# Output projection begun inside the last recurrent rounds, its weights asked for earlier, and the first key projection interleaved with the forget projection

## The chip, the cores and the metric

The kernel runs on one core of a Trainium2 chip. The metric is the device time of one execution in microseconds (us). TensorE (PE) does the matmuls and its sequencer the waits for them, VectorE (DVE) and ScalarE (ACT) do the elementwise work and read the results out of PSUM, GpSimd (POOL) scales weights and starts some transfers, and SyncE (SP) only starts transfers. Each engine runs its own instruction list in order, and the lists meet at semaphores.

## The reference, cut to what matters

```python
def rwkv7_layer(h, ...):
    xn = rmsnorm(h, norm)
    proj = token_shift(xn @ w_in, mu)              # r, k, v, z, two small ones
    ...
    y = wkv7_scan(r, decay, k, v, kk, a)           # recurrence over 1040 tokens, 16 heads of 64
    y = group_norm_per_head(y) * gn_w + gn_b
    out = (y + bonus) * silu(z)
    return h + out @ w_out                         # the output projection, then the residual

def shared_kv(h, kv_norm, kv_w, kv_f_bias, k_norm):
    kvf = rmsnorm(h, kv_norm) @ kv_w               # [k | v | 16 forget logits]
    k_sh = head_rmsnorm(kvf[..., :D], k_norm)
    v_sh = kvf[..., D:2 * D]
    log_f = log_sigmoid(kvf[..., 2 * D:] + kv_f_bias)
    c_all = cumsum(log_f, axis=1)
    return k_sh, v_sh, c_all

def fox_layer(h, k_sh, v_sh, c_all, ...):
    proj = rmsnorm(h, norm) @ w_in                 # q and z
    ...                                            # softmax(q k / 8 + c[t] - c[s]), causal, times v
    return h + (attn * silu(z)) @ w_out
```

D is 1024, the sequence has 1024 tokens and 16 meta tokens (1040 in all, padded to 1044), everything is float32. There is one recurrent layer and one attention layer.

## The kernel before

A float32 operand x is split into a high part xh (rounded to the type fp32r) and a low part xl = x - xh, likewise a weight into wh and wl, and a product of 128 channels is three matmuls: wh xh, wl xh, wh xl. The 1044 columns are taken as three segments of 348, so one channel block k (of KO = 8) against one output tile is nine matmuls, and one output tile is 72. `products` writes them. High parts are made by ScalarE (`split_hi`, `split_row`), low parts by VectorE (`split_lo`, `split_row`), and VectorE raises `w_lo` or `x_lo` when a weight or a row block is usable. Raw weights arrive in the two buffers of `wr`, asked for by SyncE in `load_w`, which waits until the previous content of the buffer has been split.

**The recurrent layer** is worked off for 8 pairs of heads times 4 segments of time, in rounds. `round_order` writes the steps of a round as one list, and every engine walks that list and picks its own work. A full round holds projections for the segment after the next, the triangular inverse of the next one ("p", "x"), and the state chain ("chain", one small matmul pair, one VectorE step, and again) of the one before. Three draining rounds follow the last full one. In the second of them, `round_order(1, False, False, True, False, False)`, only this is left: chain steps 1 to 3 of the last segment (the third is empty there), "y", the two matmul groups of the group norm "gn1" and "gn2", and "rsqrt" (Ln and Exp on ScalarE). The last round finishes the group norm on VectorE ("gn3") and stores the last segment.

A finished pair of heads is stored to `oa_scr` in DRAM. SyncE reads it back as row block k of the output projection's input (`osq`, two buffers) and it is split by `split_row`. Blocks 0 to 6 are split during the last full round ("orow" steps in `last_round_order`); block 7 only exists when the last segment is stored.

**The output projection** (tiles N_AO to N_AO + 7) starts behind the last round. Tiles 0 and 1 run side by side, channel block by channel block, in the PSUM groups G (banks 0 to 2 and 3 to 5). For tiles 2 to 7 a tile takes the buffer of the tile two before it: when tile m is finished, VectorE adds the residual (`h_t`, read back from `xt_scr`) and then splits the weight of tile m + 2. SyncE's list there is: eight loads of osq, eight loads of `h_t` (two in flight), and then the weights of tiles 2 to 7.

**Behind it** the sum of squares for the norm is closed (`over`), `normalise(1)` writes eight row blocks one after the other, and TensorE multiplies each by the 16 forget columns (tile N_F, nine matmuls for each row block, only 16 wide). Then the forget chain runs: logit, Abs, Exp, Ln, min, subtract, the cumulative sum, scale, high part, low part, alternately on VectorE and ScalarE, 16 partitions wide. GpSimd stores both parts to `c_scr` and sets the extra rows of the key and query buffers. `first_round` is the list of the steps before attention starts: key projection ("proj", 0, i), its head norm ("sumsq", "rsq", "norm"), the same for the query, "stackk", "stackq", value, and the row maxima ("smax"). Its products alternate between two PSUM banks (B_G), and ScalarE must read a bank out before the next but one product can start.

## Time and profile before

| | us |
|---|---|
| runs shown (3) | 2131.5, 2128.23, 2131.59 |
| median | 2131.5 |
| profiled execution, device time | 2133.43 |
| its span, first to last instruction | 2131.6 |
| mean granted TensorE clock, share of full | 0.966 |

TensorE is busy 92% of the span, VectorE 49%, ScalarE 44%, GpSimd 11%. The span lies 1.8 us under the profiled execution's own time. The part that the change touches lies between 1036 and 1285 us of the span: the last full recurrent round ends near 1065, the three draining rounds near 1096, tiles 0 and 1 of the output projection end at 1120, tile 7 at 1194, the first query projection at 1264. Read there which engine waits and which wait ends last; busy shares of the whole span say little about it.

### The profile page before, as it was taken

Reading aid. Unit: us, or ns where it says so; the run is one execution under the profiler, and the core shown is the slowest. Engines: PE = TensorE matmul, PEld = TensorE weight load, DVE = VectorE, ACT = ScalarE, POOL = GpSimd, SP = SyncE. Lnnn points to the kernel's source line nnn. Section 1 sums busy time; section 2 is a strip of 40 time slices with the busy share of each in tenths; the row PEclk is TensorE's granted clock in tenths of the full one; section 3 lists DMA queues with packets and bytes.
Section 4 is the critical chain, followed back from the end, with each engine's and each line's share of the span. In section 5 each row is a group of like instructions: output and inputs, shape, how many; then the busy total and the mean of one; then the engine's idle time right before and its main releaser. Section 6 shows DMA issues by size and latency. Waiting matters only on the chain.

```text
span 2131.6 us, 56907 instructions
## 1 busy us (share of the span) xinstructions
PE 1964.1 (92%) x24895; PEld 1684.4 (79%) x24895; DVE 1051.4 (49%) x1991; ACT 943.6 (44%) x1677; POOL 234.2 (11%) x261
## 2 busy tenths in 40 slices
PE   6699999999999999999889789999999999999798
PEld 4588888889898888889779577777777877777477
DVE  2646565666656665665623543343343533443521
ACT  2445454444444444454412253544555364444621
POOL 0011111111111111111000021001010101100000
PEclk9799999999999999999869898999999999999799
DMA  5101000010101000010231210010110110110233
GB/s 201 50 2 42 11 25 27 18 38 5 47 8 37 15 27 27 12 41 8 77 108 52 101 42 21 26 30 21 35 26 26 35 31 21 30 35 16 79 114 118
DMA packets 103738, 89.92 MB, mean 42 GB/s; under 512 B 4101, under 2 KB 95864, under 8 KB 103240
## 3 DMA queue, kind: packets, MB, share of 16 engines
q1 hardware_dynamic: 100120, 68.50, 10.9%
q0 software_dynamic: 3168, 17.14, 2.5%
q8 instruction: 199, 3.26, 0.6%
q10 hardware_dynamic: 208, 0.66, 0.1%
q14 instruction: 43, 0.35, 0.1%
HBM read 64.96 MB, written 21.33 MB: 40 GB/s over the span
## 4 chain that ended last, share of the span: by engine, by line
PE 74%; DVE 9%; ACT 9%; issue 5%; DMA 2%; SPq 0%; ACTq 0%; DVEq 0%; POOLq 0%
PE ps L1711 6%; PE ps L2024 6%; PE ps L2026 5%; PE ps L2025 5%; PE ps L1713 5%; PE ps L1712 5%; PE ps L2107 5%; PE ps L1815 4%; PE ps L1647 3%; PE ps L1649 3%; PE ps L1648 3%; PE ps L1844 2%; PE ps L2060 2%; PE ps L2088 2%; PE ps L1839 2%
## 5 line engine op out<-in xcount | busy, mean ns | idle before, releaser
L1711 PE MATMUL ps<-xh,wh 128*128 128x258 f32 (+1 forms) x1024 | 328.0, 320 | 7.5 <-ACT arena L887 3.5
L1712 PE MATMUL ps<-xh,wl 128*128 128x258 f32 (+1 forms) x1024 | 291.2, 284 | 0.0
L1713 PE MATMUL ps<-xl,wh 128*128 128x258 f32 (+1 forms) x1024 | 291.0, 284 | 0.0
L2024 PE MATMUL ps<-xh,wh 128*128 128x348 f32 x768 | 262.3, 341 | 8.4 <-ACT arena_b L1075 5.2
L2025 PE MATMUL ps<-xh,wl 128*128 128x348 f32 x768 | 248.5, 324 | 0.0
L2026 PE MATMUL ps<-xl,wh 128*128 128x348 f32 x768 | 248.3, 323 | 0.0
L1711 PEld LDWEIGHTS ps<-xh,wh 128*128 128x128 f32 x1024 | 193.6, 189 | 26.0 <-ACT arena L887 6.0
L1591 DVE TENSOR_REDUCE arena_b<-ps 128x1 f32<-128x144 f32 (+4 forms) x224 | 106.2, 505 | 192.8 <-PE ps L2064 176.3
L1712 PEld LDWEIGHTS ps<-xh,wl 128*128 128x128 f32 x1024 | 194.3, 190 | 2.6
L1713 PEld LDWEIGHTS ps<-xl,wh 128*128 128x128 f32 x1024 | 193.6, 189 | 0.0
L1075 ACT ACTIVATE arena_b<-ps 128x348 f32<-128x348 f32 x96 | 43.9, 458 | 293.8 <-PE ps L2026 293.8
L2107 PE MATMUL ps<-arena_b 128*128 128x512 f32 (+4 forms) x448 | 164.3, 483 | 4.7 <-ACT arena_b L1160 4.7
L858 ACT ACTIVATE arena<-ps,pp 128x257 f32<-128x257 f32 (+1 forms) x128 | 61.3, 479 | 230.1 <-PE ps L1713 230.1
L1647 PE MATMUL ps<-xh,wh 128*128 128x348 f32 (+2 forms) x368 | 133.0, 361 | 28.2 <-DVE xl L1208 21.3
L2024 PEld LDWEIGHTS ps<-xh,wh 128*128 128x128 f32 x768 | 146.7, 191 | 13.8 <-ACT arena_b L1075 5.5
L2025 PEld LDWEIGHTS ps<-xh,wl 128*128 128x128 f32 x768 | 146.3, 190 | 4.5 <-issue 0.3
L2026 PEld LDWEIGHTS ps<-xl,wh 128*128 128x128 f32 x768 | 145.8, 190 | 0.0
L1200 DVE TENSOR_TENSOR wl<-wr,wh 128x1024 fp32r<-128x1024 f32 (+1 forms) x50 | 60.1, 1204 | 154.8 <-ACT wh L1038 98.7
L1648 PE MATMUL ps<-xh,wl 128*128 128x348 f32 (+2 forms) x368 | 131.4, 357 | 0.0
L1649 PE MATMUL ps<-xl,wh 128*128 128x348 f32 (+2 forms) x368 | 131.2, 357 | 0.0
L1408 DVE TENSOR_TENSOR arena<-ps,levels 128x256 f32<-128x256 f32 (+1 forms) x192 | 86.9, 452 | 78.3 <-PE ps L1815 77.4
L1815 PE MATMUL ps<-arena 64*64 64x64 f32 x2880 | 121.1, 226 | 2.9 <-DVE arena L1421 2.9
(255 smaller groups left out, 4357.4 us busy)
## 6 DMA issues: line engine op xcount, KB each, us to landing
wr<-in_w_in SPq DMA_DIRECT2D x33, 512.0 KB, 4.1
xt_scr<-arena POOLq DMA_DIRECT2D x2, 4176.0 KB, 13.3
wr<-in_kv_w SPq DMA_DIRECT2D x16, 512.0 KB, 3.9
wr<-in_b_w_in SPq DMA_DIRECT2D x16, 512.0 KB, 3.9
arena<-xt_scr SPq DMA_DIRECT2D x8, 522.0 KB, 4.7
arena<-oa_scr SPq DMA_DIRECT2D x8, 520.0 KB, 3.7
arena<-in_x SPq DMA_DIRECT2D x8, 512.0 KB, 3.4
wr<-in_w_out SPq DMA_DIRECT2D x8, 512.0 KB, 3.8
```

Of the source, the lines that this page charges most:

```text
L1591: dve.tensor_reduce(mpart[:, 3 * t + part:3 * t + part + 1], ps[:, B_SM[i % 2], 0:k1 - k0], AX.X, ALU.max).then_inc(S.smax, 1)
L1647: pe.matmul(acc, wh[:, slot, k, 0:width], xh[:, k, t], start=(k == 0), stop=False)
L1648: pe.matmul(acc, wl[:, slot, k, 0:width], xh[:, k, t], start=False, stop=False)
L1649: mm = pe.matmul(acc, wh[:, slot, k, 0:width], xl[:, k, t], start=False, stop=(k == KO - 1))
L1711: pe.matmul(bank, wh[:, j, k, :], xh[:, k, t], start=(k == 0), stop=False)
L1712: pe.matmul(bank, wl[:, j, k, :], xh[:, k, t], start=False, stop=False)
L1713: mm = pe.matmul(bank, wh[:, j, k, :], xl[:, k, t], start=False, stop=(k == KO - 1))
L1815: mm = pe.matmul(ps[to[c], B_P, x * CH:(x + 1) * CH], am_[hc, e, j, A_BA], xs[hc, 0, x, :] if l else ident[hc, hc], start=(l > 0), stop=Tr ...
L2024: pe.matmul(bank[:, 0:SEG], wh[:, slot, k, :], xh[:, k, t], start=(k == 0), stop=False)
L2025: pe.matmul(bank[:, 0:SEG], wl[:, slot, k, :], xh[:, k, t], start=False, stop=False)
L2026: mm = pe.matmul(bank[:, 0:SEG], wh[:, slot, k, :], xl[:, k, t], start=False, stop=(k == KO - 1))
L2107: pe.matmul(ps[:, B_PV[qb_], q0 - 512 * qb_:512], vflat[e][0:n_k, kt, :], pt[n_ % 4][0:n_k, 0:n_q], start=(kt == 0), stop=(kt == 4 * qb_ + 4),
```

## The change

There are four edits.

- `tail_order` puts 14 pieces ("ao", m, k) into the second draining round: channel blocks 0 to 6 of output tiles 0 and 1, nine matmuls each. One stands behind each of the steps chain 1, chain 2, chain 3, "y" and "gn1", the other nine at the round's end. Only channel block 7 of both tiles is left behind the rounds. The output projection uses the banks GO (1 to 3 and 4 to 6), so that banks 0 and 7 stay with the recurrence.
- SyncE asks for the weights of tiles 2 and 3 behind the osq loads 3 and 4, not behind the eight loads of `h_t`.
- The first key projection leaves `first_round` on TensorE and runs with the forget projection, row block by row block, three segments in banks 0 to 2. Its weight is split before `normalise(1)` on both engines.
- The forget chain is a step of `first_round` now, behind the key's head norm. GpSimd scales the value weight before it waits for the chain's end, not after it.

```diff
+        def tail_order():
+            pieces = [("ao", m, k) for k in range(KO - 1) for m in range(2)]
+            steps = []
+            for st_ in round_order(1, False, False, True, False, False):
+                steps.append(st_)
+                if st_[0] in ("chain", "y", "gn1"):
+                    steps.append(pieces.pop(0))
+            return steps + pieces
@@ SyncE
                 sync.dma_start(osq[k % 2][:, 0:T], oa_scr[k][:, 0:T]).then_inc(O_LOADED[k % 2], 16)
+                if k in (3, 4):
+                    n = N_AO + k - 1
+                    load_w(n, wo[:, :, (k - 1) * P:k * P], n % 2, n)
...
-            for m in range(2, KO):
+            for m in range(4, KO):
                 load_w(N_AO + m, wo[:, :, m * P:(m + 1) * P], (N_AO + m) % 2, N_AO + m)
@@ GpSimd
             scale_b(0, 1)
+            scale_b(0, 2)
             pool.wait_ge(S.c_lo, 1)
@@ ScalarE (VectorE alike)
             split_hi(n % 2, None, 1, n - 1, H)
+            split_hi((N_B + 0) % 2, None, 2, N_B - 2)
             normalise(1)
-            split_hi((N_B + 0) % 2, None, 2, N_B - 2)
-            act.wait_ge(S.f_logit, 1)
...
+                    elif kind == "forget":
+                        act.wait_ge(S.f_logit, 1)
...
@@ TensorE
+                    elif kind == "ao":
+                        m, k = st_[1:]
...
+                        pe.wait_ge(S.x_lo, KO + k + 1)
+                        products(GO[(N_AO + m) % 2], (N_AO + m) % 2, channels=[k])
...
-            pe.wait_ge(S.w_lo, N_F + 2)
+            pe.wait_ge(S.w_lo, N_B + 2)
+            pe.wait_ge(S.h_ln, 2)
             for k in range(KO):
                 pe.wait_ge(S.x_lo, 2 * KO + k + 1)
                 mm = products(G[N_F % 2], N_F % 2, H, channels=[k])
...
+                for i in range(3):
+                    t = slice(i * SEG, (i + 1) * SEG)
+                    pe.matmul(G[0][:, i, :], wh[:, N_B % 2, k, :], xh[:, k, t], start=(k == 0), stop=False)
+                    pe.matmul(G[0][:, i, :], wl[:, N_B % 2, k, :], xh[:, k, t], start=False, stop=False)
+                    mm = pe.matmul(G[0][:, i, :], wh[:, N_B % 2, k, :], xl[:, k, t], start=False, stop=(k == KO - 1))
@@ first_round
-            return (of(0) + [("sumsq", 0, i) for i in range(3)] + [("rsq", 0), ("norm", 0)]
+            return (of(0) + [("sumsq", 0, i) for i in range(3)] + [("rsq", 0), ("norm", 0), ("forget",)]
```

Lines of the changed kernel lie some 17 further down on TensorE. TensorE's list in the second draining round, before the change (L1932 is a chain step, L1944 "y", L1955 and L1962 the group norm, L1647 the first matmul of the output projection; a row with "waits" waits for those semaphores):

```order
L1932 MATMUL ps<-arena 64x64 [waits s_ready]
L1932 MATMUL ps<-arena 64x64
L1944 MATMUL ps<-arena 64x64 [waits s_ready,rp_ready]
L1944 MATMUL ps<-arena 64x64 x7
L1955 MATMUL ps<-arena,head_ones 128x256 [waits y_added]
L1962 MATMUL ps<-arena,head_ones 128x256 [waits gn_sq,gn_centred]
L1647 MATMUL ps<-xh,wh 128x348 [waits gn_centred,x_lo,gn_rstd,w_lo]
```

The same place of the changed kernel, to the end of "gn2" (L1949 is a chain step, L1961 "y", L1980 and L1987 the group norm, L1664 the first of nine matmuls of a piece, of which the other eight are left out each time):

```order
L1949 MATMUL ps<-arena 64x64 [waits s_ready]
L1949 MATMUL ps<-arena 64x64
L1664 MATMUL ps<-xh,wh 128x348 [waits x_lo]
...
L1664 MATMUL ps<-xh,wh 128x348 [waits x_lo]
...
L1961 MATMUL ps<-arena 64x64 [waits s_ready,rp_ready]
L1961 MATMUL ps<-arena 64x64 x7
L1664 MATMUL ps<-xh,wh 128x348 [waits x_lo]
...
L1980 MATMUL ps<-arena,head_ones 128x256 [waits y_added]
L1664 MATMUL ps<-xh,wh 128x348 [waits x_lo]
...
L1987 MATMUL ps<-arena,head_ones 128x256 [waits gn_sq,gn_centred]
```

So five pieces stand inside the chain and the group norm, and the wait for the group norm's end (gn_rstd) moved behind all fourteen.

ScalarE's list from the closing of the norm's statistics, before the change (L793 a weight's high part, L806 and L808 the norm's Ln and Exp, L811 the row blocks, L1026 to L1032 the forget chain, L1075 reading a projection out, L1089 the Ln behind "sumsq"):

```order
L793 ACTIVATE wh<-wr 128x8x16 [waits proj_done,w_scaled]
L806 ACT_TABLE_LOAD [waits setup_dve]
L811 ACTIVATE xh<-arena 128x1044 [waits xn_mul] x8
L793 ACTIVATE wh<-wr 128x1024 [waits proj_done,w_scaled]
L1026 ACTIVATE arena_b<-arena_b 16x1044 [waits f_logit]
L1028 ACTIVATE arena_b<-arena_b 16x1044 [waits f_abs]
L1032 ACTIVATE wh<-arena_b 16x1044 [waits c_scaled]
L793 ACTIVATE wh<-wr 128x1024 [waits proj_done,w_scaled]
L1075 ACTIVATE arena_b<-ps 128x348 [waits b_done] x3
L1089 ACTIVATE arena_b<-ps,cst 128x348 [waits b_done] x3
```

The same of the changed kernel (L807 a weight's high part, L825 the row blocks, L1082 reading a projection out, L1096 the Ln, L1109 to L1115 the forget chain, L1044 the value weight's high part):

```order
L807 ACTIVATE wh<-wr 128x1024 [waits proj_done,w_scaled]
L825 ACTIVATE xh<-arena 128x1044 [waits xn_mul] x8
L1082 ACTIVATE arena_b<-ps 128x348 [waits b_done] x3
L1096 ACT_TABLE_LOAD
L1096 ACTIVATE arena_b<-ps,cst 128x348 [waits b_done] x3
L1109 ACTIVATE arena_b<-arena_b 16x1044 [waits f_logit]
L1111 ACTIVATE arena_b<-arena_b 16x1044 [waits f_abs]
L1115 ACTIVATE wh<-arena_b 16x1044 [waits c_scaled]
L1044 ACTIVATE wh<-wr 128x1024 [waits b_done,w_scaled]
L1082 ACTIVATE arena_b<-ps 128x348 [waits b_done] x3
```

The forget chain moved from ahead of reading out the key projection to ahead of reading out the query projection.

## Rows read from the trace of the kernel before

**Rows 1.** The page's first part: engine, busy us, share, instructions.

```profile
PE 1964.1 (92%) x24895; PEld 1684.4 (79%) x24895; DVE 1051.4 (49%) x1991; ACT 943.6 (44%) x1677; POOL 234.2 (11%) x261
```

**Rows 2.** Windows: from:to, us, each engine's busy us (instructions), PEclk, DMA share, GB/s.

```profile
1085.51:1091.31 5.80, 3.29 (x26) 2.09 (x27) 2.65 (x7) 0.54 (x2) 0.54 (x1) 0.50 0.07 24
...
1094.84:1099.33 4.49, 4.49 (x16) 4.49 (x17) 1.33 (x3) 0.00 (x0) 0.54 (x1) 0.50 0.09 33
1099.33:1120.08 20.75, 20.75 (x130) 20.46 (x129) 2.49 (x2) 1.08 (x1) 0.00 (x0) 1.00 0.85 270
...
1123.78:1126.55 2.77, 2.77 (x9) 2.77 (x10) 2.76 (x3) 1.67 (x2) 0.00 (x0) 0.50 0.59 168
...
1136.85:1194.30 57.45, 57.36 (x360) 57.07 (x359) 17.04 (x15) 9.65 (x9) 0.40 (x1) 1.00 0.11 29
```

**Rows 3.** Timeline of TensorE: start, us, line, operation, operands, [idle before, releaser].

```profile
1085.51 0.48 PE L1932 MATMUL ps<-arena 64*64 64x64 f32 x4 [0.47 <-DVE arena L1452]
...
1091.31 1.19 PE L1962 MATMUL ps<-arena,head_ones 128*128 128x256 f32 x2 [1.06 <-ACT arena L984]
```

**Rows 4.** Chain of waits, 1000 to 1300: "y" and "gn1" in a full round.

```profile
1019.74 0.42 PE ps L1944 x16
...
1023.24 0.66 PE ps L1955 x2
```

**Rows 5.** Chain of waits, 1087 to 1124: start, us, what; then VectorE's timeline.

```profile
1096.54 2.03 DMA oa_scr<-arena
...
1099.48 5.27 DMA arena<-xt_scr
...
1114.45 6.93 DMA wr<-in_w_out
...
1103.30 1.25 DVE L1296 TENSOR_TENSOR xl<-arena,xh 128x1044 fp32r<-128x1044 f32 x1 [7.06 <-ACT xh L838]
```

**Rows 6.** Timeline of VectorE behind tile 2: residual, then a weight's low part.

```profile
1136.88 1.25 DVE L1507 SCALAR_TENSOR_TENSOR arena<-ps,arena 128x1044 f32<-128x1044 f32 x1 [9.62 <-PE ps L1649]
1138.04 1.22 DVE L1200 TENSOR_TENSOR wl<-wr,wh 128x1024 fp32r<-128x1024 f32 x1
```

**Rows 7.** Timeline of TensorE: first matmul of tile 2 of the output projection.

```profile
1123.78 0.66 PE L1647 MATMUL ps<-xh,wh 128*128 128x348 f32 x1 [3.69 <-DVE wl L1200]
```

**Rows 8.** Chain of waits in the last full round: osq load 4.

```profile
1050.71 3.86 DMA arena<-oa_scr
```

**Rows 9.** Timelines of TensorE, VectorE (twice) and GpSimd at the norm's first row blocks.

```profile
1210.74 0.45 PE L1647 MATMUL ps<-xh,wh 128*16 128x348 f32 x1 [7.36 <-DVE xl L1208]
...
1210.63 2.83 DVE L1217 TENSOR_TENSOR arena<-arena 128x1044 f32<-128x1044 f32 x1
1213.38 1.23 DVE L1208 TENSOR_TENSOR xl<-arena,xh 128x1044 fp32r<-128x1044 f32 x1
...
1210.30 2.05 POOL L666 TENSOR_TENSOR wr<-wr,params 128x1024 f32<-128x1024 f32 x1 [12.00 <-DMA wr<-in_b_w_in]
```

**Rows 10.** Timelines of ScalarE (forget chain, key, query) and TensorE.

```profile
1231.28 1.08 ACT L1026 ACTIVATE arena_b<-arena_b 16x1044 f32<-16x1044 f32 x1 [3.58 <-DVE arena_b L1525]
...
1248.37 0.46 ACT L1075 ACTIVATE arena_b<-ps 128x348 f32<-128x348 f32 x1 [5.37 <-PE ps L2026]
...
1254.30 1.08 ACT L1103 ACTIVATE arena_b<-arena_b 128x1044 f32<-128x1044 f32 x1
...
1263.91 0.46 ACT L1075 ACTIVATE arena_b<-ps 128x348 f32<-128x348 f32 x1 [3.35 <-PE ps L2026]
...
1265.49 1.28 ACT L1089 ACT_TABLE_LOAD   x1
...
1242.71 0.64 PE L2024 MATMUL ps<-xh,wh 128*128 128x348 f32 x1 [5.21 <-ACT arena_b L1075]
```

**Rows 11.** Timelines of GpSimd (last of eight memsets) and ScalarE's queue ("stackk").

```profile
1251.52 1.87 POOL L753 MEMSET qc<- 1x1044 f32 x2
...
1268.93 0.48 ACTq L1117 DMA_DIRECT2D kb<-c_scr  x1
```

More of the change, by code:

```diff
@@ L762, in store_ob @@
                 pool.sem_inc(S.ob_free, 1)
-            for j in range(2, 4):
-                scale_b(0, j)
+            scale_b(0, 3)
             scale_b(1, 0)
@@ L1995, in _ @@
                     pe.wait_ge(S.res_added, m - 1)
[L1996 removed]
+                products(GO[n % 2], n % 2).then_inc(S.proj_done, 1)
             pe.wait_ge(S.res_added, KO)
@@ L2009, in round_pe @@
                     kind = st_[0]
+                    if first and st_[0:2] == ("proj", 0):
+                        continue
                     if kind in ("proj", "sumsq", "vrow"):
@@ L2013, in round_pe @@
                         bank = ps[:, B_G[local % 2], :]
-                        if not (first and local < L_K + 2) and st_[3:] != (1,):
+                        if st_[3:] != (1,):
                             pe.wait_ge(S.b_evac, chunk(p, local) - 1)
```

81 lines of the change are left out of this document (43 added, 38 removed).

## The prediction

> **What bounds the kernel now.** First the page's first part: TensorE is busy 92% of the span [rows 1]. The 8% left is where a change of order can pay, so the second view is the timeline of TensorE with what ended its idle times, and the third is the chain of waits at those places. Between 1085 and 1264 us there are three holes. The first is the draining rounds: a chain step lasts 0.48 and TensorE then waits 0.47 for VectorE, the group norm waits for ScalarE [rows 3], and the output projection starts only at 1094.84, at the low clock. The second is tile 2's weight: TensorE waits 3.69 [rows 7], because the weight was asked for at 1114.45, behind the residual's loads, and took 6.93 to land [rows 5]. The third is the forget chain: ScalarE works it off in its order and cannot read the key projection out, so TensorE waits 5.21 for a bank [rows 10].
>
> The windows give two prices for a 348-column matmul. At a granted clock of 0.50 (1.2 GHz) 16 take 4.49 and 9 take 2.77: 0.29 each. At 1.00 (2.4 GHz) 360 take 57.45: 0.16 each. After 1094.84 the clock rose 4.5 after the dense matmuls began, after 1123.78 2.8 after [rows 2]. I take 4.4.
>
> **Part one, the 14 pieces.** They remove nothing, 126 matmuls only move. Before, tiles 0 and 1 end at 1120.08 [rows 2]. After, on the same clock of the trace: the second chain step starts at 1085.51 [rows 3], the first piece 0.2 behind it. Three pieces (27 matmuls) and a chain step are 15 at 0.29, 12 at 0.16 and 0.2: 6.5, to 1092.2. "y" 0.42 [rows 4], a piece 1.44, "gn1" 0.66 [rows 4], a piece 1.44, "gn2" 0.66: to 1096.8. Each of these steps waits for VectorE or ScalarE, but those waits (0.47, 1.06) are shorter than a piece. Before, "gn2" ended at 1092.5 [rows 3]. So the group norm's end, the store and the reload come 4.3 later: channel block 7 is ready at 1104.55 + 4.3 = 1108.9 [rows 5]. Meanwhile nine pieces (81 x 0.16 = 13.0) run until 1109.8, so block 7 is just covered, by 0.9. Its two parts end at 1111.2 and 1112.7.
>
> **Part two, the weight of tile 2.** It is there now, so behind tile 0 only residual and low part stand: from 1136.85 to 1139.26, 2.4 [rows 2, 6]. Tile 2 starts at 1113.6, after an idle time of 0.9 in place of 3.69, and I take its clock as still up: 72 x 0.16 = 11.5, end 1125.1. Before it ended at 1136.85 [rows 2]. Gain of both parts: 11.7. What is late next: h_t's first load, asked for 4.3 later, lands at 1099.48 + 5.27 + 4.3 = 1109.1 [rows 5], 2.1 ahead of its use at 1111.2. The weights of tiles 4 and 5 come some 4 later than h_t's last load did, but TensorE needs tile 4's only after tiles 2 and 3, 23.0 behind 1113.6. Both have cover.
>
> The cost is in the last full round, where SyncE's queue now has tile 2's weight ahead of osq load 4. That load is on the chain of waits there with its whole 3.86 [rows 8], and ScalarE stands in order behind it. From above: an equal load asked for just behind another took 5.27 in place of 3.86 [rows 5, 8], 1.4 more. From below nothing, since the weight goes out some 3.4 earlier and may be through. Nothing makes the load faster, so no gain. I take the middle, 0.7, since 3.4 of lead is near a transfer's 3.86 but short of it. Tile 3's weight meets osq loads 5 and 6, which stand under the same bound. Gain so far 11.0.
>
> **Part three, the key projection with the forget projection.** Before, TensorE starts the forget blocks at 1210.74 [rows 9] and ScalarE reads out the last key segment at 1248.37 [rows 10]. After, each row block brings 18 matmuls: the first costs 15 x 0.29 + 3 x 0.16 = 4.8, to 1215.6; the others 2.9 each, more than the 2.4 in which VectorE makes a block, so TensorE is the bound. Block 1 was ready at 1213.38 + 1.23 = 1214.6 [rows 9]. There is a clash: GpSimd's scaling from 1210.30 to 1212.35 stretched VectorE's multiply to 2.83 [rows 9], ending 1.1 behind it, and the value weight's scaling (2.05) now follows at once. Block 1 comes at 1216.7, the eighth is multiplied at 1216.7 + 7 x 2.88 = 1236.8.
>
> The Trainium skill, GPSIMD Engine Reference, Specifications, says that GpSimd shares its SBUF interfaces with VectorE and contends with instructions of two SBUF inputs. That speaks against moving this scaling, and the stretched multiply of [rows 9] agrees. Without it the sum of this part would be 1.1 better (1215.6 + 7 x 2.88 = 1235.7).
>
> ScalarE splits the query weight in between (1.06), and ends reading out at 1237.7 against 1248.83: 11.1 earlier. The norm's Ln now needs a table load that the forget chain's Ln paid for before; 1.28 less the 1.0 that "sumsq" takes: 0.3. The key's Exp ends at 1255.38 - 10.8 = 1244.6 [rows 10]. Now the forget chain stands: from its Abs to TensorE's restart 11.43 (1231.28 to 1242.71), so 1256.0. Meanwhile TensorE has done two query segments (48 x 0.16 = 7.7, from 1252.4 - 10.8 = 1241.6, where 1252.4 is the restart behind "sumsq", 4.0 behind the readout of [rows 10]) and waits 6.7 for a bank. The third, at the low clock as the key's was (1242.71 to 1248.37, 5.66), ends at 1261.7 in place of 1263.9 [rows 10]. The stall was moved, not removed: of 10.8 gained 2.2 stay, and 0.3 more, as the query's Ln finds its table (a load of 1.28 at 1265.49, partly covered). Part three: 2.5; bounds 1.0 and 4.0 (a longer clash; none, and a faster rise).
>
> The end of the chain also moves GpSimd's stores and eight memsets: before done at 1253.4 [rows 11], 10.7 behind TensorE's restart of [rows 10], now about 1266.7. ScalarE's "stackk" asks for them at 1268.93 - 2.5 = 1266.4 [rows 11]: no cover where there were 15, but ScalarE's data path is at the query's Exp for some 2 more, so I cost it at nothing. The scaling of the query layer's last weight, queued on GpSimd behind the memsets, has cover of the same size.
>
> **Sum.** 11.0 + 2.5 = 13.5. The profiled execution took 2133.43, which gives 2119.9; it lay 1.9 above the median 2131.5, on which the prediction stands: 2118.0.
>
> **The rivals.**
> 1. *The key's gain is wholly lost.* The forget chain or GpSimd's memsets are a little later than worked out, and "stackk" waits, with ScalarE's reading out behind it. For: the memsets have a cover of about 2 where they had 15. Against: value products give ScalarE some slack. Gain 11.0: 2120.5.
> 2. *The clock rises only behind "gn2".* For: it stood at 0.50 from 1085.51 to 1091.31 with TensorE busy for 3.29 of 5.80 [rows 2], and small steps lie between the first pieces. Then the 45 matmuls of the first five pieces cost 13.1 in place of 9.2 (15 at 0.29, 30 at 0.16), and "y", "gn1", "gn2" twice their 1.7: 5.6 later for all behind. Against: nothing idles between the pieces. Gain 13.5 - 5.6 = 7.9: 2123.6.
> 3. *Slower than before.* The clock stays at 1.2 GHz through all pieces: 144 x 0.29 and 3.7 for the small steps are 45.5 from 1085.7, to 1131.2 in place of 1112.7, and tile 2's first ten at 0.29 cost 1.3 more: 19.8 lost, against 13.5. Time 2131.5 + 6.3 = 2137.8. It turns from gain to loss when the rise comes later than 30 us after the forecast one (13.5 / 0.45, the share that a low clock costs). Against it: the same matmuls got 1.00 after 4.5 [rows 2].
> 4. *More than forecast.* The osq load isn't delayed, no clash, the clock rises after 2.8 as at 1123.78: 0.7, 1.1 and 1.6 x 0.45 = 0.7 more, a gain of 16.0: 2115.5.
> 5. *The change doesn't do what it says*: tile 2's weight is early only if the buffer is free and no wait holds SyncE. Its wait is for a split long done, so I fold this into rival 2.
>
> **How the numbers follow.** Forecast 0.62, rival 1 0.17, rival 2 0.10, rival 3 0.04, rival 4 0.07. The forecast's own band is its bounds: 11.0 plus or minus 0.7 and 1.0 to 4.0, so 2115.8 to 2120.2, and the runs themselves spread 3.4. From 2114.0 to 2122.5 the range holds the forecast, rival 1 and most of rival 4; it leaves out rivals 2 and 3 and a little of the others, 0.2 at most. A measurement of this kernel can tell about 0.2%, 4.3 us, from no change. Only rival 3 is slower; rivals 1 and 2 together (gain 5.4) with an unlucky spread could come within: faster 0.92, same 0.04, slower 0.04.
>
> **What the profile after would show.** Chain steps 0.2 to 3 apart with L1664 between them; a granted clock of 1.00 from about 1090; no idle time over 0.5 before block 7; tile 2's first matmul about 10 earlier, with an idle time near 1 and released by VectorE's low part. At the norm 18 matmuls for each row block and nearly no waits. In the query projection an idle time near 6.7 in front of the third segment, released by ScalarE reading out. The prediction is wrong if the clock is at 0.50 behind 1092, if block 7 is waited for, if osq load 4 lands more than 1.4 later, or if the idle time in the query projection is much shorter or longer than 6.7.

## The result and the profile after

The changed kernel takes 2117.0 us (median of 4 runs, 2115.4 to 2118.8), the kernel before, in runs beside it, 2131.2 (2128.2 to 2131.6). The ratio is 0.9935, with a 95% interval of 0.9921 to 0.9949: 14.2 us gained, where 13.5 was forecast. The profiled executions are 2133.43 before and 2118.27 after, with spans of 2131.6 and 2116.5. The 15.1 us between the spans is read below, stretch by stretch. Line numbers of TensorE's products are now L1664 to L1666 (before L1647 to L1649); the residual is L1523 (before L1507), the read-out L1082 (before L1075). The changed kernel was measured once more later, with a trace of its own; it is called the second trace below.

| milestone, us from the span's start | before | after | earlier by |
|---|---|---|---|
| ScalarE reads row 4 of the last full round | 1054.59 | 1054.72 | -0.1 |
| second chain step of the last head round | 1085.51 | 1085.16 | 0.4 |
| tile 2 of the output projection starts | 1123.78 | 1114.40 | 9.4 |
| tile 2's residual on VectorE | 1136.88 | 1126.19 | 10.7 |
| TensorE starts on the normalised input | 1210.74 | 1200.05 | 10.7 |
| third query segment read out | 1263.91 | 1250.71 | 13.2 |

**Part one and two, after.** Windows of the changed kernel, with the columns of [rows 2]: the stretch, each engine's busy time and instructions, the granted clock, the DMA share and GB/s.

```profile
1085.16:1091.08 5.92, 5.92 (x25) 5.31 (x26) 1.87 (x5) 0.00 (x0) 0.13 (x1) 0.50 0.02 4
1091.08:1113.30 22.22, 22.22 (x149) 21.60 (x148) 4.83 (x8) 6.08 (x8) 0.95 (x2) 1.00 0.38 128
1114.40:1126.15 11.75, 11.75 (x73) 11.75 (x74) 3.48 (x3) 1.95 (x2) 0.00 (x0) 1.00 0.84 250
```

Before, the stretch from the same chain step on had TensorE busy for 3.29 of 5.80 us [rows 2]. Now it is busy for all 5.92, though still at 1.2 GHz (a granted clock of 0.50), and from 1091.08 to the end of tile 1 it is busy without a break at 2.4 GHz. Tile 2's 72 matmuls, which began at the low clock before [rows 2], take 11.75.

The timeline of TensorE and VectorE there (start, us, engine and line, operation, operands, idle time before and what ended it):

```profile
1085.16 0.48 PE L1949 MATMUL ps<-arena 64*64 64x64 f32 x4 [0.47 <-DVE arena L1468]
1085.56 0.66 PE L1664 MATMUL ps<-xh,wh 128*128 128x348 f32 x1
...
1088.47 0.48 PE L1949 MATMUL ps<-arena 64*64 64x64 f32 x4
...
1092.96 0.68 PE L1961 MATMUL ps<-arena 64*64 64x64 f32 x16
...
1097.00 0.59 PE L1987 MATMUL ps<-arena,head_ones 128*128 128x256 f32 x2
...
1114.40 0.44 PE L1664 MATMUL ps<-xh,wh 128*128 128x348 f32 x1 [1.04 <-DVE wl L1216]
...
1108.60 1.25 DVE L1312 TENSOR_TENSOR xl<-arena,xh 128x1044 fp32r<-128x1044 f32 x1 [6.95 <-ACT xh L852]
1126.19 1.25 DVE L1523 SCALAR_TENSOR_TENSOR arena<-ps,arena 128x1044 f32<-128x1044 f32 x1 [8.30 <-PE ps L1666]
```

The chain step at 1088.47, "y" at 1092.96 and the second group norm at 1097.00 carry no bracket: TensorE comes to them late enough that nothing is waited for. In [rows 3] the same kinds of steps wait 0.47 and 1.06. Block 7's low part is made at 1108.60 to 1109.85 and TensorE doesn't wait for it. The wait of 3.69 for tile 2's weight [rows 7] is 1.04, ended by the low part L1216, which stands behind tile 0's residual.

**Part three, after.** The norm's first row blocks: TensorE, then VectorE and GpSimd (the place of [rows 9]).

```profile
1200.05 0.45 PE L1664 MATMUL ps<-xh,wh 128*16 128x348 f32 x1 [7.36 <-DVE xl L1224]
...
1201.10 2.94 DVE L1224 TENSOR_TENSOR xl<-arena,xh 128x1044 fp32r<-128x1044 f32 x1
1204.08 2.83 DVE L1233 TENSOR_TENSOR arena<-arena 128x1044 f32<-128x1044 f32 x1
...
1200.04 5.76 POOL L680 TENSOR_TENSOR wr<-wr,params 128x1024 f32<-128x1024 f32 x2 [12.43 <-DMA wr<-in_b_w_in]
```

Beside GpSimd's two scalings, 5.76 together, two of VectorE's operations take 2.94 and 2.83 in place of 1.25. In [rows 9] one scaling stretched one.

ScalarE from the key's norm to the key's copy for the stacking ("stackk"), then TensorE, then GpSimd (the places of [rows 10] and [rows 11]):

```profile
1227.29 1.28 ACT L1096 ACT_TABLE_LOAD   x1
...
1232.88 1.08 ACT L1119 ACTIVATE arena_b<-arena_b 128x1044 f32<-128x1044 f32 x1
1233.86 1.06 ACT L1109 ACTIVATE arena_b<-arena_b 16x1044 f32<-16x1044 f32 x1
...
1242.87 1.07 ACT L1115 ACTIVATE wh<-arena_b 16x1044 fp32r<-16x1044 f32 x1 [4.45 <-DVE arena_b L1575]
...
1250.71 0.46 ACT L1082 ACTIVATE arena_b<-ps 128x348 f32<-128x348 f32 x1 [5.14 <-PE ps L2058]
...
1255.99 0.49 ACTq L1133 DMA_DIRECT2D kb<-c_scr  x1
...
1257.62 1.06 ACT L1135 ACTIVATE ka<-arena_b 64x1044 fp32r<-64x1044 f32 x1
...
1227.41 3.56 PE L2065 MATMUL ps<-arena_b,head_ones 128*128 128x348 f32 x6 [2.02 <-ACT arena_b L1088]
...
1245.28 0.66 PE L2056 MATMUL ps<-xh,wh 128*128 128x348 f32 x1 [6.53 <-ACT arena_b L1082]
...
1254.08 1.88 POOL L768 MEMSET qc<- 1x1044 f32 x2
```

The forget chain begins at 1233.86 behind the key's Exp (1232.88), and within it ScalarE stands idle for 4.45 until VectorE's scan and scaling are through. TensorE gets its bank back at 1245.28, after an idle time of 6.53. The stall of 5.21 [rows 10] was moved, not removed.

**How the spans' 15.1 us add up.** 1.0 lies ahead of anything the change touches (VectorE's last low part of the setup is at 1036.55 before and 1035.56 after). The touched part gives 12.5, with the 0.3 of the query's Ln counted. Another 1.5 comes behind it, in a stretch whose code is the same, by where the clock is low. These are windows of 10 us, the first of the kernel before, the second of the changed one, both beginning at the same instruction:

```profile
1280.32:1290.32 10.00, 9.62 (x54) 8.94 (x55) 1.95 (x5) 1.20 (x4) 1.53 (x1) 0.83 0.00 0
```

```profile
1266.82:1276.82 10.00, 9.63 (x64) 8.94 (x65) 1.95 (x5) 1.20 (x4) 1.90 (x1) 1.00 0.04 11
```

The granted clock is 0.83 in the one and 1.00 in the other, and TensorE gets 54 matmuls done against 64. From the first copy for the key's stacking to the third it is 95.3 before and 93.8 in the changed kernel, but 93.3 in its second trace and 95.3 in a kernel with the same code there (the memsets alone, below). So the 1.5 is chance, and the forecast doesn't claim it.

### The profile page after: what moved, and what is told of

It is laid out like the page before. It is cut to its first block, busy times and chain, and to the rows that moved or that the text cites. A ratio compares the mean times of both kernels' runs of the same rounds, so it can differ in the third digit from the quotient of the medians.

```text
span 2116.5 us, 56909 instructions
## 1 busy us (share of the span) xinstructions
PE 1953.6 (92%) x24895; PEld 1677.9 (79%) x24895; DVE 1053.3 (50%) x1991; ACT 942.9 (45%) x1677; POOL 236.8 (11%) x261
## 4 chain that ended last, share of the span: by engine, by line
PE 75%; ACT 9%; DVE 9%; issue 5%; DMA 2%; SPq 0%; ACTq 0%; DVEq 0%; POOLq 0%
PE ps L1728 6%; PE ps L2056 5%; PE ps L2058 5%; PE ps L2057 5%; PE ps L1730 5%; PE ps L1729 5%; PE ps L2139 5%; PE ps L1832 4%; PE ps L1664 3%; PE ps L1666 3%; PE ps L1665 3%; PE ps L1861 2%; PE ps L2092 2%; PE ps L2120 2%; PE ps L1856 2%
## 5 line engine op out<-in xcount | busy, mean ns | idle before, releaser
L2056 PE MATMUL ps<-xh,wh 128*128 128x348 f32 x744 | 253.9, 341 | 9.8 <-ACT arena_b L1082 6.5
L2057 PE MATMUL ps<-xh,wl 128*128 128x348 f32 x744 | 239.9, 322 | 0.0
L2058 PE MATMUL ps<-xl,wh 128*128 128x348 f32 x744 | 239.8, 322 | 0.0
L1728 PEld LDWEIGHTS ps<-xh,wh 128*128 128x128 f32 x1024 | 193.4, 189 | 26.0 <-ACT arena L901 6.0
L1729 PEld LDWEIGHTS ps<-xh,wl 128*128 128x128 f32 x1024 | 194.2, 190 | 2.6
L1730 PEld LDWEIGHTS ps<-xl,wh 128*128 128x128 f32 x1024 | 193.5, 189 | 0.0
L1082 ACT ACTIVATE arena_b<-ps 128x348 f32<-128x348 f32 x96 | 43.6, 457 | 285.5 <-PE ps L2058 285.5
L2056 PEld LDWEIGHTS ps<-xh,wh 128*128 128x128 f32 x744 | 141.7, 190 | 15.4 <-ACT arena_b L1082 6.8
L1664 PE MATMUL ps<-xh,wh 128*128 128x348 f32 (+2 forms) x368 | 132.2, 359 | 20.4 <-DVE xl L1224 18.5
L2057 PEld LDWEIGHTS ps<-xh,wl 128*128 128x128 f32 x744 | 141.2, 190 | 4.4 <-issue 0.3
L2058 PEld LDWEIGHTS ps<-xl,wh 128*128 128x128 f32 x744 | 140.6, 189 | 0.0
L1216 DVE TENSOR_TENSOR wl<-wr,wh 128x1024 fp32r<-128x1024 f32 (+1 forms) x50 | 60.1, 1205 | 152.7 <-ACT wh L1044 99.1
L1666 PE MATMUL ps<-xl,wh 128*128 128x348 f32 (+2 forms) x368 | 129.8, 353 | 0.0
```

The costliest lines, as they stand in the source:

```text
L1664: pe.matmul(acc, wh[:, slot, k, 0:width], xh[:, k, t], start=(k == 0), stop=False)
L1666: mm = pe.matmul(acc, wh[:, slot, k, 0:width], xl[:, k, t], start=False, stop=(k == KO - 1))
L1728: pe.matmul(bank, wh[:, j, k, :], xh[:, k, t], start=(k == 0), stop=False)
L1729: pe.matmul(bank, wl[:, j, k, :], xh[:, k, t], start=False, stop=False)
L1730: mm = pe.matmul(bank, wh[:, j, k, :], xl[:, k, t], start=False, stop=(k == KO - 1))
L2056: pe.matmul(bank[:, 0:SEG], wh[:, slot, k, :], xh[:, k, t], start=(k == 0), stop=False)
```

## The experiments

Ten runs in three groups, each group measured together with the kernel before on one chip. Four stand beside 2132.7 us for the kernel before: weights behind the residual, no pieces, the key part alone, weights behind load 6. Four stand beside 2131.2: pieces behind the second group norm, the forget chain in two, that with the memsets ahead, and that with two smaller mends. The last two, the memsets alone and the changed kernel again, stand beside 2132.3. I use differences between medians of one group, and traces from the same instruction to the same instruction, since two stretches whose code no edit changes vary by 2 to 3.5 us (last section).

### What the early weights, the pieces and their place are worth

**Weights behind the residual again.** The pieces and the key part stay.

```diff
-                if k in (3, 4):
-                    n = N_AO + k - 1
-                    load_w(n, wo[:, :, (k - 1) * P:k * P], n % 2, n)
...
-            for m in range(4, KO):
+            for m in range(2, KO):
```

> The changed kernel, but the weights of output tiles 2 and 3 are asked for behind the eight residual loads again. Theory: the pieces alone are worth nothing or worse, because they delay the group norm by about 5 us, with it the residual loads, and tile 2's weight stands behind those. The last residual load is asked for at about 1119.3 on the changed kernel's clock, the weight takes 6.9 to land, then 2.3 for its high and low part: tile 2 starts near 1128.6 in place of 1114.4, and starts at the low clock (1.3 more), while osq load 4 lands 0.6 earlier. So about 15 slower than the changed kernel, near 2132, no faster than the kernel before. Rival: the pieces carry most of the gain by themselves and the early weight only its own stall of 2.8 and a cold start of 1.3: then about 4 slower than the changed kernel, near 2121.

Measured: 2135.1 (12 runs, 2129.6 to 2139.6), ratio 1.0005 (0.9996 to 1.0014). ScalarE, TensorE and SyncE's transfer (chain of waits) in this kernel:

```profile
1127.14 1.06 ACT L804 ACTIVATE wh<-wr 128x1024 fp32r<-128x1024 f32 x1 [19.09 <-DMA wr<-in_w_out]
...
1129.51 0.66 PE L1661 MATMUL ps<-xh,wh 128*128 128x348 f32 x1 [16.73 <-DVE wl L1213]
```

```profile
1119.44 7.68 DMA wr<-in_w_out
```

TensorE is done with tiles 0 and 1 as early as in the changed kernel, and then waits 16.73 us. Worse, the weight is asked for at 1119.44, 35.0 behind the second chain step (1084.46 here), where before it was 28.9 behind it [rows 3, 5]. The pieces delay the group norm's end, with it the last load of its rows, and with that everything that stands behind this load on SyncE. By the traces, the stretch from the second chain step to TensorE's start on the normalised input is 133.2 here and 125.2 before. So the pieces without the early weights lose 8 us there. Part of it comes back behind it, where the key part brings its gain.

**No pieces, early weights kept.** The output projection's first two tiles run behind the group norm as before (their waits and products move back there on TensorE, not shown), the rest is as changed.

```diff
-            pieces = [("ao", m, k) for k in range(KO - 1) for m in range(2)]
-            steps = []
-            for st_ in round_order(1, False, False, True, False, False):
-                steps.append(st_)
-                if st_[0] in ("chain", "y", "gn1"):
-                    steps.append(pieces.pop(0))
-            return steps + pieces
+            return round_order(1, False, False, True, False, False)
```

> The changed kernel without the pieces: channel blocks 0 to 6 of tiles 0 and 1 stand behind the rounds and behind the wait for the group norm again. The early weights and the key part stay. Theory: tiles 0 and 1 end near 1119.4 in place of 1113.3, tile 2 follows after 1 us, so 6 to 6.5 slower than the changed kernel: near 2123.3. Rival (early weight is all there is, the pieces are hidden by the wait for channel block 7): within 1 of the changed kernel.

Measured: 2124.3 (5 runs), ratio 0.9960 (0.9947 to 0.9973). TensorE at tile 2:

```profile
1118.13 0.43 PE L1658 MATMUL ps<-xh,wh 128*128 128x348 f32 x1 [1.04 <-DVE wl L1210]
```

From its second chain step (1082.41) to tile 2 it takes 35.7, against 29.2 in the changed kernel and 38.3 before: the pieces are worth 6.5 there, as expected.

**The key part alone.** Both edits above together.

> The kernel before with the key part alone (key projection beside the forget one, forget chain as a step behind the key's norm, value weight scaled earlier); neither pieces nor early weights. Theory: the stall only moved to the query projection, 2.5 to 2.8 faster than the kernel before: near 2128.5. Rival (the key projection's earlier end counts in full): 10 or more faster, near 2121; second rival (nothing comes through): within 0.7 of the kernel before.

Measured: 2130.6 (11 runs), ratio 0.9990 (0.9982 to 0.9999), 2.0 us below the kernel before in the same group, where 2.5 to 2.8 was expected. In its trace the stretch from TensorE's start on the normalised input to its restart for the third query segment is 45.5 (1207.35 to 1252.82), against 45.2 in the changed kernel.

With these three the parts can be added up, all in one group: key part alone 2130.6; with the early weights 2124.3, so 6.3 for the weights; with the pieces too 2119.5 (the run with the weights behind load 6, below, which differs from the changed kernel only in where they are asked for), so 4.8 for the pieces. But with the pieces and late weights it is 2135.1: there the pieces cost 4.5. Their sign hangs on the weights. By the traces the weights' share is smaller than by the medians: from the second chain step to the start on the normalised input the weights bring 3.3 (124.7 to 121.4). Of this 1.8 is tile 2's start, and the rest is tile 2 itself, whose first 3 us have a granted clock of 0.54 with the late weight and 1.00 with the early one. The two profiled executions differ by 3.6 in all, since the one of the key part alone is the fastest of its 11 runs. The rest of the 6.3 I can't place; the two ratios' intervals leave 3 us of room on either side.

**All pieces behind the second group norm**, instead of between its steps.

```diff
                 steps.append(st_)
-                if st_[0] in ("chain", "y", "gn1"):
-                    steps.append(pieces.pop(0))
             return steps + pieces
```

> All 14 pieces stand directly behind the second group norm instead of between the chain steps, y and the first group norm; nothing else differs from the changed kernel. Theory (the pieces pay twice: they fill TensorE's waits and they lift its clock before the group norm): the group norm ends some 4.5 us earlier than in the changed kernel, as before the change (1092.5 against 1097.0), but the first pieces then run at the low clock with nothing hidden, so tiles 0 and 1 end later: 14 pieces from 1092.5 with 4.5 us of clock rise are 16 x 0.29 + 110 x 0.16 = 22.2 us, to 1114.8, then block 7's 18 matmuls 2.9, to 1117.7, against 1113.4 in the changed kernel. So some 4 us slower than the changed kernel: near 2121, ratio to the kernel before 0.9953. Rival (the place does not matter, only that they run before block 7 is there): within 1 us of the changed kernel, ratio 0.9935. Against no pieces at all (2124.3, ratio 0.9960) the theory expects 2 to 3 us faster.

Measured: 2119.7 (5 runs), ratio 0.9947 (0.9933 to 0.9961). TensorE:

```profile
1083.27 0.33 PE L1947 MATMUL ps<-arena 64*64 64x64 f32 x4 [0.52 <-DVE arena L1466]
...
1115.83 0.43 PE L1662 MATMUL ps<-xh,wh 128*128 128x348 f32 x1 [1.04 <-DVE wl L1214]
```

32.6 from the second chain step to tile 2: 3.3 more than the changed kernel, 3.2 less than without pieces. (The seven traces with the pieces between the steps and the weights early lie between 28.1 and 29.3.) So about half of the pieces' gain is that they run while block 7 is on its way through memory, and half that they stand between the chain steps. How much of that second half is filled waits and how much is an earlier rise of the clock, no run takes apart. The rival, that the place doesn't matter, falls in the trace; the ratios alone (0.9947 and 0.9935) would not tell.

### The transfer that the early weights delay

**Weights asked for behind load 6** of the group norm's rows, instead of behind loads 3 and 4.

```diff
-                if k in (3, 4):
-                    n = N_AO + k - 1
-                    load_w(n, wo[:, :, (k - 1) * P:k * P], n % 2, n)
+                if k == 6:
+                    for n in (N_AO + 2, N_AO + 3):
+                        load_w(n, wo[:, :, (n - N_AO) * P:(n - N_AO + 1) * P], n % 2, n)
```

> The changed kernel, but the weights of tiles 2 and 3 are asked for behind osq load 6, where no osq load follows for some 45 us. Theory: osq load 4 lands after 3.9 in place of 4.7, the last full round is 0.6 to 0.8 shorter, all behind is earlier by that: 0.7 faster than the changed kernel, near 2116.4; ScalarE's wait for osq load 4 falls from 1.05 to about 0.2. Rival (that load's delay is covered): ScalarE's wait falls and the time stays.

Measured: 2119.5 (6 runs, 2113.3 to 2121.1), ratio 0.9931 (0.9919 to 0.9943). Too near 0.9935 to tell. The timeline of ScalarE tells it: row 1's and row 4's copies, first in the kernel before, then in the changed one, then in this one.

```profile
1044.59 1.06 ACT L838 ACTIVATE xh<-arena 128x1044 fp32r<-128x1044 f32 x1
...
1054.59 1.07 ACT L838 ACTIVATE xh<-arena 128x1044 fp32r<-128x1044 f32 x1 [0.20 <-DMA arena<-oa_scr]
```

```profile
1043.88 1.06 ACT L852 ACTIVATE xh<-arena 128x1044 fp32r<-128x1044 f32 x1
...
1054.72 1.08 ACT L852 ACTIVATE xh<-arena 128x1044 fp32r<-128x1044 f32 x1 [1.05 <-DMA arena<-oa_scr]
```

```profile
1045.65 1.06 ACT L852 ACTIVATE xh<-arena 128x1044 fp32r<-128x1044 f32 x1
...
1055.73 1.07 ACT L852 ACTIVATE xh<-arena 128x1044 fp32r<-128x1044 f32 x1 [0.28 <-DMA arena<-oa_scr]
```

10.00, 10.84 and 10.08 from the one to the other. The weight ahead of load 4 costs 0.84 there, and behind load 6 it costs nothing. All twelve traces agree: 10.8 to 11.2 in the seven with the weights behind loads 3 and 4, 9.8 to 10.1 in the five others. The cost reaches the chain nearly whole. From row 1 to the second chain step the three take 40.92, 41.28 and 40.94, but over all twelve traces it is 41.2 to 42.0 with the weights there (mean 41.5) and 40.4 to 40.9 without (mean 40.8), so some 0.7. That is below what a comparison of whole runs can show.

### The stall that was moved

In the changed kernel the next thing in the way is the forget chain. Behind it stand two waits: ScalarE can't read out the first query segment while it waits for VectorE's scan, and the key's stacking waits for GpSimd, whose stores and eight memsets follow the chain's end. Four kernels take these apart: the chain cut in two, the memsets moved, both, and neither.

**The forget chain in two.** ScalarE's last copy and VectorE's low part become a step of their own behind the first query segment's read-out.

```diff
             return (of(0) + [("sumsq", 0, i) for i in range(3)] + [("rsq", 0), ("norm", 0), ("forget",)]
-                    + of(1) + [("sumsq", 1, i) for i in range(3)] + [("rsq", 1), ("norm", 1)]
+                    + proj(1, 0) + [("forget2",)] + proj(1, 1) + proj(1, 2) + [("sumsq", 1, i) for i in range(3)] + [("rsq", 1), ("norm", 1)]
...
                         act.activation(f_a[0:H, :], f_a[0:H, :], ACT.Ln, bias=1.0).then_inc(S.f_ln, 1)
+                    elif kind == "forget2":
                         act.wait_ge(S.c_scaled, 1)
...
+                    elif kind == "forget2":
                         dve.wait_ge(S.c_hi, 1)
```

> The forget chain is cut in two steps: ScalarE's last copy (which waits 4.45 us for VectorE's scan) and VectorE's low part stand behind the first query segment's read-out, so that ScalarE reads the segment out first. Theory: TensorE's idle time of 6.5 us before the third query segment falls to about 1.1 us, but nearly all of that is given back at the next wait: ScalarE then stands before the key's stacking, which waits for GpSimd's eight memsets (they end at 1256.0 in the changed kernel, behind the forget chain's end). Gain 1 us: near 2116, ratio 0.9930. Rival (the idle time of TensorE is itself the loss): 5 to 7 us faster than the changed kernel, near 2111, ratio 0.9905.

Measured: 2116.6 (5 runs), ratio 0.9938 (0.9924 to 0.9951). TensorE, ScalarE and GpSimd:

```profile
1238.57 0.43 PE L2058 MATMUL ps<-xh,wh 128*128 128x348 f32 x1 [1.13 <-ACT arena_b L1082]
...
1255.96 1.07 ACT L1136 ACTIVATE ka<-arena_b 64x1044 fp32r<-64x1044 f32 x1 [5.98 <-POOL qc L768]
...
1253.52 1.87 POOL L768 MEMSET qc<- 1x1044 f32 x2
```

TensorE's idle time falls from 6.53 to 1.13, and next to nothing comes of it: ScalarE now waits 5.98 for the memsets, with the next weight and its read-outs queued behind. This copy comes 56.5 behind TensorE's start on the normalised input, 1.1 earlier than in the changed kernel's first trace (57.6) and 2.2 earlier than in its second (58.7), and the ratio shows no gain. The rival, that TensorE's idle time is itself the loss, is ruled out.

**The same, with the memsets ahead** of GpSimd's wait for the chain's low part.

```diff
-            pool.wait_ge(S.c_lo, 1)
-            pool.dma_start(c_scr[:, 0, :], f32(chi[0:H, :])).then_inc(S.c_stored, 16)
-            pool.wait_ge(S.c_stored, 16)
-            pool.dma_start(c_scr[:, 1, :], f32(clo[0:H, :])).then_inc(S.c_stored, 16)
             pool.wait_ge(S.h_stored, 16)
...
             pool.wait_ge(S.setup_bp, 8)
+            pool.wait_ge(S.c_lo, 1)
+            pool.dma_start(c_scr[:, 0, :], f32(chi[0:H, :])).then_inc(S.c_stored, 16)
+            pool.wait_ge(S.c_stored, 16)
+            pool.dma_start(c_scr[:, 1, :], f32(clo[0:H, :])).then_inc(S.c_stored, 16)
             pool.wait_ge(S.c_stored, 32)
```

> As e5_forget_in_two, and GpSimd's eight memsets stand ahead of its wait for the forget chain's low part instead of behind its two stores. Theory: the key's stacking then waits only for the two stores (the second lands near 1250 on the changed kernel's clock), which is no later than the query's norm, so the gain of the cut is kept: the key's copy at 1251.7 in place of 1257.6, 5 to 6 us faster than the changed kernel: near 2111.5, ratio 0.9908. Rival (memsets beside VectorE's work of 1224 to 1236 stretch its operations as GpSimd's scaling does, and the key's norm or the query's low weight comes later): 2 us or less faster than the changed kernel.

Measured: 2108.0 (4 runs, 2105.5 to 2111.0), ratio 0.9893 (0.9878 to 0.9909). That is 8.6 below the kernel with the cut alone.

```profile
1238.18 0.43 PE L2058 MATMUL ps<-xh,wh 128*128 128x348 f32 x1 [1.12 <-ACT arena_b L1082]
...
1223.04 1.87 POOL L764 MEMSET qc<- 1x1044 f32 x2
...
1249.80 1.08 ACT L1136 ACTIVATE ka<-arena_b 64x1044 fp32r<-64x1044 f32 x1 [0.21 <-issue]
```

The memsets are over by 1225, where nobody needed GpSimd, and ScalarE's copy for the key's stacking follows the Exp directly. From TensorE's start on the normalised input to this copy it takes 51.5 (1198.35 to 1249.80), 56.5 in the run before it and 57.6 in the changed kernel (1200.05 to 1257.62): 6.1 less. The rival, a clash of the memsets with VectorE, was hardly put to the test: from 1217.46 to 1224.91, while they ran, VectorE had three short operations, which took 1.29, 0.54 and 0.54 as in the changed kernel.

**The memsets alone**, the forget chain whole.

> The changed kernel with GpSimd's eight memsets ahead of its wait for the forget chain's low part, and the forget chain whole. Theory (the cut and the memsets' place pay only together: the two waits stand in parallel ahead of the key's stacking): the memsets' end at 1256.0 was hidden behind the query's norm, which ends there by the third query segment's lateness, so moving it alone brings at most the 0.6 us by which the rows leave room: within 1 us of the changed kernel, ratio 0.993 to 0.9935. Rival (the memsets were the bound by themselves, and the cut adds little): most of the 6 us of the two together, ratio near 0.991.

Measured: 2118.4 (5 runs), ratio 0.9933 (0.9919 to 0.9947).

```profile
1242.67 0.66 PE L2056 MATMUL ps<-xh,wh 128*128 128x348 f32 x1 [6.63 <-ACT arena_b L1082]
...
1256.31 1.07 ACT L1135 ACTIVATE ka<-arena_b 64x1044 fp32r<-64x1044 f32 x1
```

TensorE's idle time is the changed kernel's, and the copy comes 58.5 behind the start on the normalised input (1197.84), which is within what the changed kernel does (57.6 and 58.7). The copy follows the query's Exp, and that waits for the third query segment.

**The changed kernel again**, as the base in the same group.

> The changed kernel itself, unchanged, beside the same runs of the kernel before, as the base that e8_memsets_alone is compared with on one chip. Theory and rival alike: ratio within the interval of the first measurement, 0.9921 to 0.9949, so near 0.9935. Its trace tells how much of a stretch's length comes from where the clock rises: the first pieces should again stand at 1.2 GHz for 4 to 6 us, and the last pair's attention may be up to 3.5 us longer or shorter than in the first trace.

Measured: 2119.4 (5 runs), ratio 0.9939 (0.9926 to 0.9953). So the memsets alone bring 1.0 by the medians, which their spread doesn't tell from nothing, the cut alone nothing by its ratio (0.9938), and both together some 9 to 10 by the ratios and 6 to 7 by the traces up to the key's copy. Two waits ran beside each other and ended within a us; only taking both away moves the end. In the first trace the stacking is issued at 1255.99, right when the memsets are over (1255.96). In the second they are over at 1255.73 and it is issued at 1256.68, so there the third query segment is the later one. The rest of the 9 to 10 isn't explained: the last stretch of the kernel, whose code is the same, is 3.5 us shorter in the traces of all three kernels with the chain in two (last section).

The third segment of the two traces, its window from TensorE's restart to the read-out, the first trace first:

```profile
1245.28:1250.71 5.43, 5.39 (x24) 5.10 (x24) 1.19 (x1) 0.29 (x2) 3.23 (x5) 0.73 0.47 121
```

```profile
1245.06:1251.97 6.91, 6.88 (x24) 6.59 (x24) 1.18 (x1) 0.29 (x1) 4.72 (x7) 0.55 0.38 95
```

The same 24 matmuls take 5.43 at a granted clock of 0.73 and 6.91 at 0.55.

**With two smaller mends**: the weights behind load 6, and the third scaling on GpSimd behind the norm's last low part, so that one scaling and not two meets VectorE there (only the second is shown).

```diff
             scale_b(0, 1)
-            scale_b(0, 2)
             pool.wait_ge(S.h_stored, 16)
             pool.wait_ge(S.x_lo, 3 * KO)
+            scale_b(0, 2)
             pool.wait_ge(S.w_scaled, 4)
```

> As e6_memsets_ahead, and two smaller mends: the weights of tiles 2 and 3 are asked for behind load 6 of the group norm's rows in place of loads 3 and 4 (ScalarE waited 1.05 us for load 4 in place of 0.20), and the third scaling on GpSimd stands behind the last low part of the normalised input, so that only one scaling clashes with VectorE's work there. Theory: 0.8 + 0.3 to 0.5 us faster than e6_memsets_ahead: near 2110.5, ratio 0.9903. Rival: the load's wait lies beside other work, then no more than 0.3 us from e6_memsets_ahead.

Measured: 2107.5 (4 runs, 2107.3 to 2108.8), ratio 0.9890 (0.9875 to 0.9905). From TensorE's start on the normalised input to the copy for the key's stacking it is 50.4, 1.1 less than the kernel with the cut and the memsets ahead, and from the setup's last low part to the second chain step 49.2 in place of 50.2. But the ratio can't tell the two apart. By the ratios this version is 23.4 us below the kernel before and 9.6 below the changed one.

## Why the prediction was right, step by step

**The first pieces: direction and mechanism right, 1.1 us too early.** The pieces fill the waits and the clock rises among them, as said. It didn't stay low until "gn2" (rival 2) or through all pieces (rival 3). But "y" comes 7.8 behind the second chain step (1085.16 to 1092.96), where 6.7 was worked out. The term that was mis-sized is "15 at 0.29, 12 at 0.16 and 0.2". The clock rose 5.5 behind the first piece, not 4.4, so 17 matmuls ran at the low clock (the window's 25 instructions less the 8 of two chain steps): 0.3. The other 0.8 is at the seams: the first piece starts 0.40 behind its chain step and the next one 0.41 behind 1088.47, where 0.2 was taken for each, and a piece's first matmul holds TensorE for 0.46 (1085.56 to 1086.02) in place of 0.29. From "y" to the end of the second group norm it is 4.6, as worked out.

**Cover of block 7: right, but thin.** It was ready 24.7 behind the second chain step instead of 23.4, but the pieces ended 25.2 behind it instead of 24.3, and TensorE didn't wait. The cover was 0.5, not 0.9. The weights of the later tiles, which the prediction held to be covered, were: ScalarE stood idle 10.54 for tile 4's, and TensorE never.

**Tile 2: right but for what came before it.** Idle 1.04 in place of 0.9, clock up, 11.75 in place of 11.5. From the second chain step to tile 2's residual the gain is 10.3 where 11.7 was worked out.

**The osq load: right.** It cost 0.84 of ScalarE's time, between the bounds 0 and 1.4, against 0.7 taken. The transfer itself took 4.70 in place of 3.86 [rows 8]:

```profile
1050.00 4.70 DMA arena<-oa_scr
```

From the setup's last low part to the second chain step the changed kernel took 49.60, the one before 48.96, so 0.6 is the charge of this trace, and the twelve traces above put it at some 0.7. Parts one and two together: 10.3 - 0.6 = 9.7, where 11.0 was forecast. The 1.3 is mostly the 1.1 of the first pieces.

**Part three: the sum right, by two errors that cancel in this trace.** From tile 7's residual to the third query segment's read-out the gain is 2.5 (10.69 earlier before it, 13.20 behind it) and 0.3 more for the Ln, against 2.5 in all. The key was read out 0.8 earlier than worked out: TensorE was on row block 0 until 1204.6, much of it at the low clock (0.59 granted), so it didn't wait for block 1, and for block 2 only 0.53. But "sumsq" then ran at the low clock and took 3.56 instead of the 2.3 it takes at 2.4 GHz:

```profile
1227.41:1230.97 3.56, 3.56 (x7) 2.05 (x8) 1.52 (x3) 2.26 (x3) 0.00 (x0) 0.54 0.08 19
```

The prediction named no such term. In the changed kernel's second trace the same step begins at 1228.13 at the full clock, after the same idle time of 2.02, so the fall is chance. There block 1 was waited for, 1.32 where 1.1 was worked out, the key's Exp ended within 0.4 of the forecast, and it was the third segment that went wrong, by the low clock: 6.91 in place of 5.66. Part three gained only 1.4 and 0.3 in that trace, within the bounds of 1.0 and 4.0. The forget chain to TensorE's restart took 11.42 (11.43 forecast), the idle time 6.53 (6.7), the third segment 5.43 (5.66). "Moved, not removed" was the sentence on which this part stood, and it held.

The clash of two scalings was worked out as 2.05 more on GpSimd with VectorE stretched until it ends. The trace has both engines slower: GpSimd needed 5.76 for the two scalings, not 4.1, and VectorE's two operations took 2.9 and 2.8. In the second trace it is 4.76 for the scalings and 2.98 and 2.94 for VectorE:

```profile
1200.08 4.76 POOL L680 TENSOR_TENSOR wr<-wr,params 128x1024 f32<-128x1024 f32 x2 [12.31 <-DMA wr<-in_b_w_in]
...
1200.11 2.98 DVE L1233 TENSOR_TENSOR arena<-arena 128x1044 f32<-128x1044 f32 x1
```

The difference is who came first: there GpSimd began at 1200.08 and VectorE at 1200.11, while in the first trace VectorE had begun at 1199.94 and GpSimd came at 1200.04. The durations fit engines that take turns, operation by operation, which is a reading and not shown by itself. The Trainium skill, GPSIMD Engine Reference, Specifications, says that the two contend where a VectorE instruction reads two SBUF inputs, and the trace agrees: 3.3 us lost on VectorE, some 1.7 on GpSimd. Of this only about 0.5 reached TensorE in the first trace and 1.3 in the second.

**What was missed.** 9.7 + 2.8 = 12.5 is the touched part, 1.0 less than the 13.5. The median gained 14.2. The difference of 1.7 is within what the untouched stretches do between runs; the changed kernel measured again gave a ratio of 0.9939, which is 13.0. Its trace gives 11.1 for the touched part, against the one trace of the kernel before. So the mechanism was right and the forecast for the touched part 1.0 to 2.4 too high, and it is luck that the total came within 1 us of it. The rival "the key's gain is lost to the memsets" was close: the memsets ended at 1255.96, and ScalarE issued the key's stacking at 1255.99. The experiments show that this was a second wait beside the first, and nearly as long.

## What to carry to other kernels

Work that is moved into an engine's waits pays only if what it delays has its own inputs early: with the weights late, the same pieces were no gain, because the load of the next weight stood on the queue behind the one that the pieces delayed. When a stall is taken away and the time stays, look for a second wait that ends within a us of it, and take both; here the ratios show nothing for the cut alone and for the memsets alone, and together they brought 6 us or more. Independent fills such as memsets belong ahead of an engine's wait, not behind it.

## What the runs showed of the hardware

**Two places of equal code vary by 2 and by 3.5 us.** From the second pair of heads to the last, the copies for the key's stacking follow each other by 38.7 and 55.9 us in turn, the same within 0.1 in every trace. But from the first copy to the third it is 93.3 to 95.4. And the last stretch, from the last such copy to the end, is 159.2 before, 159.2 and 158.6 in the two traces of the changed kernel, 157.3 in three others (no pieces, pieces behind the second group norm, key part alone) and 155.7 in all three kernels with the forget chain in two. Whether the cut itself brings these 3.5 us or they are chance, no run here tells. The granted clock tells what differs. TensorE's windows there (us, busy, clock, DMA share, GB/s), in the changed kernel and then in the one with the forget chain in two, from 30 us behind that copy:

```profile
1987.30:1997.30 10.00, 9.32 (x29) 0.58 0.30 107
1997.30:2007.30 10.00, 5.50 (x13) 0.66 0.12 28
```

```profile
1986.10:1996.10 10.00, 5.78 (x29) 1.00 0.37 121
1996.10:2006.10 10.00, 8.57 (x26) 0.83 0.12 28
```

The 29 matmuls keep TensorE busy for 9.32 at a clock of 0.58 and for 5.78 at 1.00. An experiment worth 1 us is read between two instructions of a trace, not from whole runs.

**The clock doesn't rise or fall at the same point each time.** It rose 5.5 behind the first piece in one trace of the changed kernel and 4.6 in the other (1086.13 to 1090.77). Behind the same idle time of 2.02 ahead of "sumsq" it was at 1.2 GHz in the one and at 2.4 GHz in the other.

**A table load costs its own time only.** In the changed kernel the last Ln ends at 1231.57, the load takes 1.28, and the Exp starts at 1232.88 (shown above):

```profile
1231.02 0.55 ACT L1096 ACTIVATE arena_b<-ps,cst 128x348 f32<-128x348 f32 x1 [0.61 <-PE ps L2065]
1231.59 1.28 ACT L1119 ACT_TABLE_LOAD   x1
```

The Trainium skill, ScalarE: Activation LUTs, What ACT_TABLE_LOAD costs, gives 1283 ns for the load and some 1380 ns more for a drain. The trace agrees with the first and not with the second: there is no such gap on either side of the load.
